# Moving attention head steps between matmul chunks, regrouping the second layer's query and key columns, and moving one weight split

## The reference

```
h = rmsnorm(x, norm_mix[i])
layer 0: q, k, v, qm = split(h @ w_in_a)      # 12 query heads, 4 key heads, 4 memory-query heads, 64 wide
         softmax(q k^T/8 - slope*|t-s|, within 128 tokens, with a sink logit) v
layer 1: q, k, v, qm = split(h @ w_in_b)      # 12 query, 12 key, 12 value heads, 4 memory-query heads
         softmax(q k^T/8 + a learned bias in a 16-column window) v
both:    softmax(qm mk^T/8) mv                # 4 heads over 256 memory tokens
x = x + concat(y_tok, y_mem) @ w_out[i]
x = x + (silu(gate) * up) @ w_down[i]
```

## Time and profile before

| | |
|---|---|
| median of 3 runs (lowest, highest) | 1080.51 us (1079.98, 1080.86) |
| profiled execution, its own time | 1080.16 us |
| its span in the profile | 1078.2 us |
| granted TensorE clock, mean | 0.986 |
| PE, DVE, ACT, POOL busy | 1020.3, 731.9, 571.0, 116.6 us |
| layer 0: tiles, bare stretch, output product | about 33 to 79.6, 79.6 to 102.4, 102.4 to 138.6 us |
| layer 1: the same | about 350 to 391.9, 391.9 to 412.4, 412.4 to 446.2 us |

### The profile page before, as it was taken

How to read it: one execution, slowest core, us unless ns; L and a number is a source line. 1 busy time by engine, 2 the same in 40 slices (tenths; PEclk the granted TensorE clock), 3 DMA queues, 4 the chain that set the end, 5 groups by cost and what they waited for, 6 DMA issues and landing times.

```text
span 1078.2 us, 14197 instructions
## 1 busy us (share of the span) xinstructions
PE 1020.3 (95%) x5572; PEld 864.3 (80%) x5572; DVE 731.9 (68%) x986; ACT 571.0 (53%) x818; POOL 116.6 (11%) x168
## 2 busy tenths in 40 slices
PE   6897999999999989899999999997999999999996
PEld 5675877889888777788888777886877789999885
DVE  5567774665356567578888667769776757778753
ACT  6657554344345557544444435577746465655541
POOL 0112140000000022200000011013550000000001
PEclk9999999999999999999999999999999999999998
DMA  9765479665565431389999796545365527555531
GB/s 350 280 167 73 135 192 284 209 195 176 169 202 194 146 128 41 117 287 353 335 337 323 277 326 225 173 149 168 127 205 206 174 90 227 193 187 167 174 137 40
DMA packets 108433, 214.03 MB, mean 199 GB/s; under 512 B 5440, under 2 KB 33360, under 8 KB 104976
## 3 DMA queue, kind: packets, MB, share of 16 engines
q1 hardware_dynamic: 103664, 196.39, 54.0%
q0 software_dynamic: 4416, 16.51, 6.4%
q10 hardware_dynamic: 288, 0.23, 0.1%
HBM read 208.39 MB, written 6.15 MB: 199 GB/s over the span
## 4 chain that ended last, share of the span: by engine, by line
PE 66%; DVE 12%; ACT 10%; DMA 7%; issue 5%; POOL 0%; DVEq 0%; SPq 0%; ACTq 0%; POOLq 0%
PE bank L899 16%; PE bank L901 16%; PE bank L900 16%; ACT hi L1216 5%; DVE lo L1651 4%; PE bank L916 4%; PE bank L917 4%; PE bank L918 4%; DMA raw<-in_w_gate_up 3%; PE bank L875 3%; DMA raw<-in_w_down 2%; PE bank L928 1%; ACT junk L1087 1%; DMA raw<-in_w_in_a 1%; DVE big L1663 1%
## 5 line engine op out<-in xcount | busy, mean ns | idle before, releaser
L1651 DVE TENSOR_TENSOR lo<-raw,hi 128x2048 fp32r<-128x2048 f32 (+1 forms) x164 | 368.4, 2250 | 222.8 <-ACT hi L1216 222.5
L1216 ACT ACTIVATE hi<-raw 128x2048 fp32r<-128x2048 f32 (+1 forms) x164 | 303.5, 1854 | 246.2 <-PE bank L901 126.4
L899 PE MATMUL bank<-hi,xTh 128*128 128x512 f32 (+2 forms) x704 | 272.1, 386 | 1.7 <-DVE lo L1651 1.7
L901 PE MATMUL bank<-hi,xTl 128*128 128x512 f32 (+2 forms) x704 | 265.3, 377 | 0.0
L900 PE MATMUL bank<-lo,xTh 128*128 128x512 f32 (+2 forms) x704 | 265.1, 377 | 0.0
L899 PEld LDWEIGHTS bank<-hi,xTh 128*128 128x128 f32 x704 | 133.7, 190 | 26.3 <-DVE lo L1651 2.3
L901 PEld LDWEIGHTS bank<-hi,xTl 128*128 128x128 f32 x704 | 133.3, 189 | 24.8
L900 PEld LDWEIGHTS bank<-lo,xTh 128*128 128x128 f32 x704 | 133.7, 190 | 22.5
L899 PE MATMUL bank<-hi,hTh 128*128 128x512 f32 x264 | 103.3, 391 | 1.2 <-DVE lo L1651 1.2
L901 PE MATMUL bank<-hi,hTl 128*128 128x512 f32 x264 | 102.8, 389 | 0.0
L900 PE MATMUL bank<-lo,hTh 128*128 128x512 f32 x264 | 102.8, 389 | 0.0
(11 more groups left out here) (351 smaller groups left out, 1415.3 us busy)
## 6 DMA issues: line engine op xcount, KB each, us to landing
raw<-in_w_gate_up SPq DMA_DIRECT2D x44, 1024.0 KB, 6.7
raw<-in_w_down SPq DMA_DIRECT2D x30, 1024.0 KB, 5.1
raw<-in_w_ada SPq DMA_DIRECT2D x24, 1024.0 KB, 7.2
raw<-in_w_up SPq DMA_DIRECT2D x22, 1024.0 KB, 5.1
raw<-in_w_in SPq DMA_DIRECT2D x21, 1024.0 KB, 5.2
raw<-in_w_out SPq DMA_DIRECT2D x12, 1024.0 KB, 5.1
raw<-in_w_in_b SPq DMA_DIRECT2D x10, 1024.0 KB, 5.1
raw<-in_w_in_a SPq DMA_DIRECT2D x6, 1024.0 KB, 11.9
```

The source lines that it names most:

```text
L899: e.matmul(o, sh, h[:, k, :], start=p.first and k == 0, stop=False)
L901: done = e.matmul(o, sl, h[:, k, :], start=False, stop=p.last and k == p.nk - 1)
L1216: e.activation(hi_s[m % SPLITS][:, 0:n], raw[p.at % RAWS][:, 0:n], ACT.Copy).then_inc(hi_made, 1)
L1651: e.tensor_tensor(lo_s[s][:, 0:n], raw[p.at % RAWS][:, 0:n], hi_s[s][:, 0:n].bitcast(F), ALU.subtract).then_inc(lo_made, 1)
```

## The change

- Layer 0: the last tile (columns 0) pops 2, 2 and 1 entries between its chunks, where it popped 1, 1, 1, and the memory tile pops 2 at each of its three places, where it popped 1. Its 15 remaining steps are now put into the queue by the table and not after the loop; the order of the queue stays.
- Layer 1: the tiles are worked off as 2048, 1536, 0, 512, 1024. The columns of `w_in_b` are reordered on the host, so that each of the last three tiles holds the queries and the keys of the same four heads (8 to 11, 0 to 3, 4 to 7). `PAIRS`, `STAGED` and the kinds follow. The last two tiles pop 2, 2, 1.
- Both layers: no split is asked for within the last output part; split 17 (and 65) stands behind that part's addition, the two transposes of it and its squares.

```diff
-MIX_TILES = [[(1024, 4, [2, 2, 1]), (512, 4, [2, 2, 1]), (0, 0, 1)], [(2048, 4, 2), (1536, 0, 1), (512, 0, 1), (1024, 4, 1), (0, 0, 1)]]
+MIX_TILES = [[(1024, 4, [2, 2, 1]), (512, 4, [2, 2, 1]), (0, 15, [2, 2, 1])],
+             [(2048, 4, 2), (1536, 0, 1), (0, 4, 1), (512, 4, [2, 2, 1]), (1024, 11, [2, 2, 1])]]
...
-         (1, 512): [(0, "q", 4, 0.125), (256, "k", 0, 1.0)],
-         (1, 1024): [(0, "k", 2, 1.0), (256, "k", 4, 1.0)],
-         (1, 0): [(0, "q", 0, 0.125), (256, "q", 2, 0.125)]}
-STAGED = [[1024, 512, 0], [2048, 512, 1024, 0]]
+         (1, 0): [(0, "q", 4, 0.125), (256, "k", 4, 1.0)],
+         (1, 512): [(0, "q", 0, 0.125), (256, "k", 0, 1.0)],
+         (1, 1024): [(0, "q", 2, 0.125), (256, "k", 2, 1.0)]}
+STAGED = [[1024, 512, 0], [2048, 0, 512, 1024]]
...
-            self.linear("mem", 1, 0, 512, 2, "mem", 1)
+            self.linear("mem", 1, 0, 512, 2, "mem", 2)
...
+                self.hold = k == 1 and n == 1
                 self.part(made[n], ("y", l), k == 0, k == 1, self.pop)
                 if k == 1:
                     self.evacuate(made[n])
                 self.pop(3)
         self.drain()
+        self.hold = False
+        self.split_through(self.owed - 1)
...
+    x = given["w_in_b"]
+    spans = [(512, 768), (1280, 1536), (0, 256), (768, 1024), (256, 512), (1024, 1280), (1536, x.shape[-1])]
+    given["w_in_b"] = np.ascontiguousarray(np.concatenate([x[..., i:j] for i, j in spans], axis=-1))
```

More of the change, by code:

```diff
@@ L454, in mix @@
     def mix(self, l):
-        kinds = {0: {1024: "vm", 512: "k", 0: "q"}, 1: {2048: "vm", 1536: "v", 512: "q", 1024: "q", 0: "q"}}[l]
+        kinds = {0: {1024: "vm", 512: "k", 0: "q"}, 1: {2048: "vm", 1536: "v", 0: "q", 512: "q", 1024: "q"}}[l]
         steps = deque(("att", l, i) for i in range(23))
```

## The result

The changed kernel takes 1089.74 us (median of 4 runs, 1088.23 to 1091.01) against 1080.32 us for the kernel before in the same session: ratio 1.0078, 95% interval 1.0058 to 1.0097. It is slower by 0.8%. I had forecast 1081.2 us and no measurable change, with the range up to 1084.0. The profiled execution after took 1090.08 us, 9.92 more than that of before.

What follows compares the result with a forecast made beforehand. It took the DVE-ACT loop to pace bare head steps, with PE 95% busy. Mixing 0 + 0, splits 0.9 - 0.2, made +0.7 us: 1080.9 profiled, 1081.2 median; range 1074.8 to 1084.0, no measurable change (42%).

Steps and rivals of the forecast that it cites:

- The bare stretch and the loop: Head steps outside layer 0's tiles, paced by DVE bias, ACT exponentials, DVE sum and reciprocal: 2.66 us a head.
- The wait at 63.25: Layer 0, step 4 one chunk after the last key pair: PE arrives at 62.3 and waits 1.0 us.
- that of steps 5 and 6: Layer 0's memory tile, first place: a split ahead of job 3's reciprocal makes PE wait 2.8 us near 72.
- G = 79.6 + 6.3 + 1.0 + 2.8 = 89.7 us: Start of layer 0's bare stretch: old start, plus PE work of moved entries, plus two new waits.
- the waits together 1 us longer: Part of layer 0's lower bound, 1.5 us of loss, together with 2.9 for 2.4 us at DVE's start.
- So layer 0's mixing gains 0: Layer 0's output product starts at 102.4 us as before; bounds 4.0 us of gain, 1.5 of loss.
- The clock: Rival, 10%: the new order spares the half-clock stretch under layer 0's output product, 1.7 us go: 1079.5 us.
- 1.7 and 2.6 at the scores: Layer 1's waits at the scores of steps 8 and 12, behind the pairs they read; mixing taken as 0.
- The last split: Both layers' last part: addition waits fall to 0.85 us, part 17 stalls 1.35; layer 0 loses 0.9, layer 1 gains 0.2.
- the wait at 189.13: Layer 0: PE's 1.00 us wait for DVE after a late load, expected to shrink and pay back the stall.
- the loads fall into the table's DMAs: Rival, 21%: part 21's load, 8 to 9 us later, meets full DMA engines; +3.0 us in layer 0, 1083.3 us.
- gaps are really filled: Rival, 27%: chunks hide the head steps' latency and new waits don't come; 5.6 us faster, 1074.9 us.

Runs made afterwards that it cites:

- e1: Kernel before with layer 0's new pops alone (memory tile pops 2, 2, 2): 1084.24 us, ratio 1.0027 to before.
- e7: Kernel before with layer 1's regrouped tiles alone, the last tile popping 1, 3, 1 in place of 2, 2, 1: 1082.73 us, ratio 1.0007.
- e10: Kernel before, memory tile popping 1, 4, 1, last splits between addition and transposes, layer 1 regrouped popping 1, 3, 1, its last pairs ahead of step 11: 1076.47 us.
- e16: Kernel before with both last splits behind addition, transposes and squares, and the table's gathering DMAs bringing one head in place of twelve: ratio 1.0046 to before.
- e3: Kernel before with only the last split moved behind the addition, transposes and squares, in both layers: 1083.58 us, ratio 1.0021.
- e6: Kernel before with layer 0's new pops alone, but the memory tile popping 1, 4, 1 in place of 2, 2, 2: 1079.89 us, ratio 0.9977.
- e17: Kernel before with the table's gathering DMAs bringing one head in place of twelve, splits unmoved: ratio 1.0033 to before.

## Why the prediction was wrong

**The bare stretch and the loop: right.** From its start it took 12.56 us (12.7 forecast). The bias of job 8 came 2.2 us after it (2.4 forecast), and the next two at the loop's 2.7 us.

**Layer 0's waits: wrong, by two terms left out.** I had the memory tile end at 89.7; it ended at 94.12. The wait at 63.25 was 0.84 for 1.0, that of steps 5 and 6 1.75 for 2.8. To the 89.7 - 0.2 - 1.05 come 2.31 us of the wait for a bank and 2 x 1.7 us of half clock: 94.2. The failing step is the sum "G = 79.6 + 6.3 + 1.0 + 2.8 = 89.7 us": it has no term for the third place, behind split 13, where 2.31 us were waited, and none for the clock, 3.4 us. The two waits that it has were even too large. I had let a split block the small work behind it at the first place and not at the third, since by data step 8 needs nothing from there. I asked of every wait which data is late, and never which bank is still unread. The bound of "the waits together 1 us longer" was therefore too narrow. "So layer 0's mixing gains 0" became a loss of 4.3 us.

**The clock: in the wrong column.** I had named the very case ("a new one under the memory tile, behind the wait of 2.8, costs as much") and let it cancel against a gain. The one under the output product's matmuls was not spared (0.50 from 109.5 to 112.9 us). There were two new ones under the memory tile and one under layer 1's last tile, 5.1 us in all. In return the bare stretch of layer 0 ran at full clock, where before had 3.4 us at half; that gave next to nothing back (12.56 us for the 12.7 of the forecast), as there the loop sets the pace. e1 shows that the first of the two need not come. I treat such a stretch as a risk behind waits under a tile and not as a fixed cost; which wait brings it stays open.

**Layer 1: the waits that I summed were too large, and three terms were left out.** Forecast 1.7 and 2.6 at the scores, found 1.38 and 1.91. Not foreseen were 1.31 at 382.34 (step 4's scores behind the pairs that they read, the same pattern as I had seen for step 8), the bank's 2.33 at 398.57, and 1.7 of half clock: 5.3 us, which less 1.0 makes 4.3 of the 4.8 found, where I had taken 0. e7 and e10 show these to be the order's doing: 4.7 falls to 1.9 and to -0.3 with the same tiles.

**The last split: the stall right, what follows it wrong.** 1.25 for 1.35 in layer 0, 0.79 for 0.85 at the additions, layer 1 even for -0.2. I had counted on the wait at 189.13 to pay back and took 0.9 us in all; after has waits of 1.49 and 1.01 there, as in the rival "the loads fall into the table's DMAs", which I gave 21%. Its price of +3.0 lies near the 3.2 of the trace, in part by luck: it had a payback of 1.0 and 2.85 us of late loads where the trace has no payback and 1.6. e16 against e3 ties this part to the gathering DMAs. Why the stall survives a table 8 to 9 us later stays open.

**The rival "gaps are really filled"** came true in a form that I hadn't considered: not with this order, but with the steps at the place without a split (e6), and only for 0.9 us of the 4.0.

Altogether the mixing of both layers made 9.1 us that the sum has at 0, and layer 0's late split 3.2 for 0.9; layer 1's split and the later stages gave 2.5 back.

## What to carry to other kernels

Where several engines work off one list, small work that PE soon needs belongs where no long operation has just been put into the same queues; one place further on was worth 2 to 4 us here. For each moved instruction ask both what it reads and what must be read out of the bank that it writes. A preparation that blocks a chain is best moved by the one operation that blocks (DVE's half behind the addition, ACT's where it was), not behind the whole chain; and filling bare stretches gains little when a loop of other engines sets their pace.

## What the runs showed of the hardware

A memset on POOL held up DVE. The first rows are POOL's and the others DVE's, from e17, where a DVE `TENSOR_SCALAR` of 8 elements a row otherwise takes 0.17 us:

```profile
152.05 5.23 POOL L1934 MEMSET big<- 128x6144 f32 x1 [6.61 <-DMA scratch_rpb<-in_rpb_b]
...
152.05 0.17 DVE L1628 TENSOR_TENSOR small<-small 128x8 f32<-128x8 f32 x1
152.25 5.06 DVE L1629 TENSOR_SCALAR small<-cols 128x8 f32<-128x8 f32 x1
157.35 0.17 DVE L1630 SCALAR_TENSOR_TENSOR small<-small 128x8 f32<-128x8 f32 x1
```

It takes 5.06 us, until the memset ends at 157.28. In e16 another `TENSOR_SCALAR` beside the same memset took 5.08 us. The `TENSOR_TENSOR` of e17 that started together with the memset, at 152.05, took its usual 0.17. The splits behind it came late, PE waited 2.48 us at 159.97, and in e16 3.53 at 162.14; with half clock behind these waits PE was 4.4 and 5.6 us later than ahead of them. The Trainium skill ("SBUF — State Buffer", two separate sides) says that the two engines share a pair of ports as an exclusive lock for a whole instruction, which on DVE's side concerns its two-port modes, and operations with two SBUF inputs against a GpSimd operation that reads SBUF. The trace agrees in that the held operation ends with the memset; in which mode it ran, no row shows.

From 152 to 180 us, in which the gathering DMAs ran (the last was issued at 162.5, and none took over 16.6 us to land), the DMA engines of before were busy all the time at 234 GB/s; in e3 they were as busy from 184 to 190 and moved 355. A share of 1.0 doesn't say how much is moved.
